# Decoder trunk kernel: dilated heads scored in pairs with weight parts dealt anew, forget gates loaded with the value columns, expert sums and closing norm by tile, three output transfers

## The reference

```python
def hybrid_mixer(x, ...):                       # head groups: 4 MLA, 6 FoX, 6 dilated
    h = x @ w_in
    c_q, c_kv, k_rope, fox_qkv, fox_f, dil_qkv = jnp.split(h, cuts, axis=-1)
    ...
    log_f = jax.nn.log_sigmoid(fox_f.astype(jnp.float32) + b_forget.astype(jnp.float32))
    cum_log_f = jnp.cumsum(log_f, axis=1).transpose(0, 2, 1)
    o_b = causal_block_attention(q_b, k_b, v_b, cum_log_f)
    ...
    o_c = dilated_mixture_attention(rope(q_c, positions), rope(k_c, positions), v_c)
    return mixed @ w_out

def reference(...):
    for l in range(DEPTH):
        x = layer_norm(DEEPNORM_ALPHA * x + mix, ln_mix_g[l], ln_mix_b[l])
        xa = memory_cross_attention(x, mem, xattn_w_q[l], xattn_w_kv[l], xattn_w_o[l])
        x = layer_norm(DEEPNORM_ALPHA * x + xa, ln_mem_g[l], ln_mem_b[l])
        gates = shared_group_router(x, router_w, router_bias)
        ff = moe_ffn(x, gates, expert_w_gate[l], expert_w_up[l], expert_w_down[l])
        x = layer_norm(DEEPNORM_ALPHA * x + ff, ln_ffn_g[l], ln_ffn_b[l])
    return x
```

## Time and profile before

| | us |
|---|---|
| three timed runs: median (lowest to highest) | 868.74 (868.0 to 871.59) |
| the profiled execution's own time | 867.3 |
| its span in the trace | 865.7 |
| TensorE busy | 816.2 (94%) |
| VectorE busy | 628.9 (73%) |
| ScalarE busy | 503.0 (58%) |
| GpSimd busy | 89.9 (10%) |

### The profile page before, as it was taken

The page is one execution under the profiler, slowest core; times in us unless marked ns, Lnnn a source line. Parts: engine busy times, 40 slices in busy tenths (PEclk is TensorE's granted clock), DMA queues, the critical chain, the costliest instruction groups (busy, mean ns, idle before and its releaser), DMA issues.

```text
span 865.7 us, 12257 instructions
## 1 busy us (share of the span) xinstructions
PE 816.2 (94%) x4411; PEld 695.0 (80%) x4411; DVE 628.9 (73%) x1094; ACT 503.0 (58%) x794; POOL 89.9 (10%) x165
## 2 busy tenths in 40 slices
PE   6998899899998999999999989999999989999993
PEld 6997798679876888888889978867898768888882
DVE  4656766775657899999565577666856589999984
ACT  3655554454435788888355646544443467888871
POOL 3156200030000000000020530000200100000001
PEclk9999999999999999999999999999999999999997
DMA  9953353455333699999465524425533439999941
GB/s 275 337 178 111 128 163 106 139 160 190 94 121 121 218 366 370 364 369 372 159 181 166 180 98 146 148 97 195 196 120 100 128 118 306 366 367 366 367 147 49
DMA packets 124110, 177.06 MB, mean 205 GB/s; under 512 B 12320, under 2 KB 92720, under 8 KB 124048
## 3 DMA queue, kind: packets, MB, share of 16 engines
q1 hardware_dynamic: 122064, 169.56, 58.8%
q0 software_dynamic: 1984, 6.70, 2.6%
...
## 4 chain that ended last, share of the span: by engine, by line
PE 81%; DVE 10%; ACT 3%; issue 3%; DMA 1%; POOL 1%; SPq 0%; DVEq 0%; ACTq 0%; POOLq 0%
PE bank L1489 21%; PE bank L1491 21%; PE bank L1490 21%; DVE w_split L490 2%; PE bank L1766 2%; PE bank L1618 2%; PE bank L1659 2%; PE bank L1607 2%; PE bank L1629 1%; PE bank L1596 1%; PE bank L1650 1%; DVE xT_lo L997 1%; DVE p_sb L1046 1%; PE bank L1606 1%; DMA xs<-in_x_dram 1%
## 5 line engine op out<-in xcount | busy, mean ns | idle before, releaser
L490 DVE TENSOR_TENSOR w_split<-raw,w_split 128x1024 fp32r<-128x1024 f32 (+2 forms) x336 | 386.9, 1174 | 74.5 <-ACT w_split L485 69.9
L485 ACT ACTIVATE w_split<-raw 128x1024 fp32r<-128x1024 f32 (+2 forms) x336 | 335.5, 1010 | 111.7 <-PE bank L1491 97.5
L1489 PE MATMUL bank<-w_split,xg_hi 128*128 128x512 f32 x256 | 103.5, 404 | 0.0
L1491 PE MATMUL bank<-w_split,xg_lo 128*128 128x512 f32 x256 | 100.2, 392 | 0.0
L1490 PE MATMUL bank<-w_split,xg_hi 128*128 128x512 f32 x256 | 100.2, 391 | 0.0
L1489 PE MATMUL bank<-w_split,xT_hi 128*128 128x384 f32 (+1 forms) x224 | 77.8, 347 | 2.0 <-DVE w_split L490 1.6
L1491 PE MATMUL bank<-w_split,xT_lo 128*128 128x384 f32 (+1 forms) x224 | 75.7, 338 | 0.0
L1490 PE MATMUL bank<-w_split,xT_hi 128*128 128x384 f32 (+1 forms) x224 | 75.6, 338 | 0.0
L602 POOL TENSOR_SCALAR st<-st 128x1 f32<-128x1 f32 x12 | 5.7, 473 | 653.4 <-ACT junk L748 653.0
L707 ACT ACTIVATE qkT<-bank 66x512 f32<-66x512 f32 (+2 forms) x32 | 19.0, 593 | 80.0 <-PE bank L1596 80.0
L1491 PEld LDWEIGHTS bank<-w_split,xg_lo 128*128 128x128 f32 x256 | 48.1, 188 | 11.0
...
## 6 DMA issues: line engine op xcount, KB each, us to landing
raw<-in_expert_w_gate_dram SPq DMA_DIRECT2D x128, 256.0 KB, 5.0
raw<-in_expert_w_up_dram SPq DMA_DIRECT2D x128, 256.0 KB, 6.7
...
```

The costliest lines, as they stand in the source:

```text
L485: nc.scalar.activation(w_hi[:, i % SPL, 0:w], raw[:, i % RAW, 0:w], ACT.Copy).then_inc(hi_ready, 1)
L490: nc.vector.tensor_tensor(w_lo[:, i % SPL, 0:w], raw[:, i % RAW, 0:w], w_hi[:, i % SPL, 0:w].bitcast(F32), ALU.subtract).then_inc(lo_ready, 1)
L1489: nc.tensor.matmul(o, lhs[0], rhs[0], start=first, stop=False, skip_group_check=shared)
L1491: return nc.tensor.matmul(o, lhs[1], rhs[0], start=False, stop=last, skip_group_check=shared)
```

## The change

It has four parts. (1) The forget-gate columns, which lie behind FV's, are loaded with FV, not with A; FV comes before FK and FQ; `fz` is made from FV's banks and waited for only in the LT job. (2) The dilated heads 10 to 15 are taken in pairs: one set of transposes turns query and key of both heads (128 columns), one `head_scores` makes both heads' scores, from partitions 0 to 63 and 64 to 127, in banks `B_S` and `B_QK`; `slots` and the stream are dealt anew; VectorE divides before `evac_o`. (3) At a layer's end tile 0's sums are finished and signalled ahead of those of groups 2 and 3 of tile 1, the choice for overfull groups (`overflow`) stands ahead of the last groups, and the two tiles are added and normalized one by one, the last in halves. Parts A0 and A1 of the next layer are split before the last expert outputs are evacuated. (4) The result leaves in three transfers.

Cut to its core:

```diff
     for l in range(n_layers):
-for name, js in (("A", range(4)), ("FQ", range(4)), ("FK", range(4)), ("FV", range(2)), ("UQ", range(1)),
-                 ("UKV", range(1)), ("FV", range(2, 4)), ("DQ", range(4)), ("DK", range(4)), ("DV", range(4)),
-                 ("MK0", range(4)), ("MK1", range(4)), ("MV0", range(4)), ("WO0", range(4)), ("WO1", range(4)),
+for name, js in (("A", range(4)), ("FV", range(4)), ("FK", range(4)), ("FQ", range(2)), ("UQ", range(1)),
+                 ("UKV", range(1)), ("FQ", range(2, 4)), ("DQ", range(4)), ("DK", range(4)), ("DV", range(4)),
+                 ("MK0", range(4)), ("MK1", range(4)), ("MV0", range(4)), ("WO0", range(3)), ("WO1", range(1)), ("WO0", range(3, 4)), ("WO1", range(1, 4)),
                  ("MV1", range(4)), ("XQ0", range(4)), ("XQ1", range(4)), ("XO0", range(4)), ("XO1", range(4)),
...
-slots = [3] + [2] * 2 + [1] * 7 + [2] * 6 + [1] * 3
+slots = [3, 2, 2] + [2, 1] * 4 + [1, 2] * 2 + [1] * 4
 turns, ahead_of = [], []
...
     assert len(turns[l]) == HEADS + 3
-    ahead_of.append(turns[l][1:] + [[index[l, "WO0", 3], index[l, "WO1", 0]]])
+    ahead_of.append(turns[l][1:] + [[index[l, "WO1", 0], index[l, "WO0", 3]]])
+
+def in_pair(h):
+
+    return MLA_H + FOX_H <= h < HEADS
+
+def qk_slot(h):
+
+    return (h // 2 + 1) % 2 if in_pair(h) else h % 2
...
-    return B_QK if h >= HEADS and (h - HEADS) % 2 else B_S
+    return B_QK if (in_pair(h) or h >= HEADS) and (h - HEADS) % 2 else B_S
+
+def scored(s):
+
+    if in_pair(s - 1):
+        return (s - 1, s) if s % 2 else ()
+    return (s - 1,) if 1 <= s <= HEADS else ()
...
+    sp.wait_ge(x_ready.sem, x_ready.at(L - 1, 5))
+    sp.dma_start(out[0][0:P, :], xs[:, 0, :]).then_inc(out_sent, 16)
+    sp.wait_ge(end_half.sem, end_half.at(L - 1, 1))
+    sp.dma_start(out[0][P:2 * P, 0:DM // 2], xs[:, 1, 0:DM // 2]).then_inc(out_sent, 16)
     sp.wait_ge(x_ready.sem, x_ready.at(L - 1, 6))
-    sp.dma_start(out[0].rearrange("(t p) d -> p t d", p=P), xs[:, :, :]).then_inc(out_sent, 16)
-    sp.wait_ge(out_sent, 16)
+    sp.dma_start(out[0][P:2 * P, DM // 2:DM], xs[:, 1, DM // 2:DM]).then_inc(out_sent, 16)
+    sp.wait_ge(out_sent, 48)
...
-            nc.scalar.activation(kf[:, t, :], b[:, QR + KVR:A_ALL], ACT.Copy).then_inc(job_a.sem, 1)
-        for i in range(first + 8, first + 10):
+            nc.scalar.activation(kf[:, t, :], b[:, QR + KVR:A_W], ACT.Copy).then_inc(job_a.sem, 1)
+        for i in range(first + 8, first + 12):
             split_hi(act, i)
-
-        act.wait_ge(fz_v.sem, fz_v.at(l, 2))
+        copy_job(l, "FV", lambda t: fv[:, t, :, 0:HD], lambda b: heads_of(b, FOX_H, HD))
+
+        act.wait_ge(fz_v.sem, fz_v.at(l, 1))
         nc.scalar.activation(fz[:, 2, :], fz[:, 1, :], ACT.Exp, scale=-1.0).then_inc(fz_a.sem, 1)
...
         nc.scalar.activation(fz[:, 3, :], fz[:, 2, :], ACT.Ln, bias=1.0).then_inc(fz_a.sem, 1)
-        for i in range(first + 10, first + 12):
-            split_hi(act, i)
-        copy_job(l, "FQ", lambda t: fq[:, t, :, 0:HD], lambda b: heads_of(b, FOX_H, HD))
         for i in range(first + 12, first + 14):
...
         aT_of(l, NE - 1, 1)
+        if l + 1 < L:
+            for j in range(2):
+                split_hi(act, index[l + 1, "A", j])
...
                                                gains[:, c0:c0 + w], ALU.mult, ALU.mult).then_inc(job_v.sem, 1)
-        z3 = lambda i: fz[:, i, :].rearrange("p (t f) -> p t f", t=TT)
-        nc.vector.tensor_tensor(z3(0), kf[:, :, ROPE:], bforget[:, :].unsqueeze(1).to_broadcast([P, TT, FOX_H]),
-                                ALU.add).then_inc(fz_v.sem, 1)
-        dve.wait_ge(fz_v.sem, fz_v.at(l, 1))
+        for i in range(first + 8, first + 12):
+            split_lo(dve, i)
+        for t, b in enumerate(banks("FV")):
+            dve.wait_ge(job_a.sem, job_a.at(l, evac_a[job["FV"]] - 1 + t))
+            nc.vector.tensor_tensor(fz[:, 0, t * FOX_H:(t + 1) * FOX_H], b[:, FOX_H * HD:FOX_H * HD + FOX_H],
+                                    bforget[:, :], ALU.add).then_inc(job_v.sem, 1)
+        dve.wait_ge(job_v.sem, job_v.at(l, evac_v[job["FV"]]))
         nc.vector.scalar_tensor_tensor(fz[:, 1, :], fz[:, 0, :], -1.0, fz[:, 0, :], ALU.mult, ALU.max).then_inc(fz_v.sem, 1)
-        for i in range(first + 8, first + 10):
-            split_lo(dve, i)
+        split_lo(dve, first + 12)
         dve.wait_ge(fz_a.sem, fz_a.at(l, 2))
...
             .then_inc(fz_v.sem, 1)
-        for i in range(first + 10, first + 14):
-            split_lo(dve, i)
+        split_lo(dve, first + 13)
...
-                softmax_max(l, s - 1)
+            for h in scored(s):
+                softmax_max(l, h)
+            if in_pair(s - 1) and s % 2 == 0:
+                softmax_norm(l, s - 1)
             if 2 <= s <= HEADS + 1:
                 evac_pT(l, s - 2)
+            if 1 <= s <= HEADS and not (in_pair(s - 1) and s % 2 == 0):
+                softmax_norm(l, s - 1)
             if s >= 3 and (s - 3) % 2 == 1:
...
                 evac_o(l, s - 3)
-            if 1 <= s <= HEADS:
-                softmax_norm(l, s - 1)
...
                 dve.nop().then_inc(s_.sem, s_.per)
-        add_experts(l)
+        add_experts(l, 0)
         scale(l, 2, 0)
-        rest_of_norm(l, 2)
+        add_experts(l, 1)
+        norm_x(l, 2, 0)
+        scale(l, 2, 1)
+        norm_halves(l, 2, 1, end_half)
...
         d = MLA_D if h < MLA_H else FOX_D if h < MLA_H + FOX_H else DIL_D
-        if h >= MLA_H + FOX_H:
+        if in_pair(h):
+            pe.wait_ge(s_masked.sem, s_masked.at(l, 2 * h))
             pe.nop().then_inc(paused_t, 1)
...
                 c0 = (2 * n + t) * P
-                ins = nc.tensor.transpose(B_QK[0:d, c0:c0 + P], v[:, t, g, :], ident[:, :])
-        ins.then_inc(qk_done.sem, 1)
+                if in_pair(h):
+                    ins = nc.tensor.transpose(B_QK[:, c0:c0 + P], v[:, t, g:g + 2, :].rearrange("p h d -> p (h d)"),
+                                              ident[:, :])
+                else:
+                    ins = nc.tensor.transpose(B_QK[0:d, c0:c0 + P], v[:, t, g, :], ident[:, :])
+        ins.then_inc(qk_done.sem, 2 if in_pair(h) else 1)
...
     def head_scores(l, h):
-        if h < HEADS:
+        if in_pair(h):
+            pe.wait_ge(qkT_ready.sem, qkT_ready.at(l, h + 2))
+            pe.wait_ge(s_masked.sem, s_masked.at(l, 2 * h))
+            for q, k in ((slice(0, P), slice(0, P)), (slice(P, T), slice(P, 3 * P))):
+                for i in range(2):
+                    v = qkT[i * DIL_D:(i + 1) * DIL_D, qk_slot(h), :]
+                    ins = nc.tensor.matmul(score_bank(h + i)[:, k], v[:, q], v[:, T:T + k.stop - k.start],
+                                           start=True, stop=True)
+            ins.then_inc(s_done.sem, 2)
+        elif h < HEADS:
...
                                            stop=g == NG - 1 and v is y_lo, skip_group_check=True)
-        if t == TT - 1 and g == NG - 1:
+        if g == NG - 1:
             ins.then_inc(summed.sem, 1)
...
         if l:
-            keep_busy(27)
+            keep_busy(20)
         if l == 0:
...
         if l:
-            keep_busy(3)
+            keep_busy(5)
+            pe.wait_ge(end_half.sem, end_half.at(l - 1, 1))
+            for f in range(KC):
+                if f == KC // 2:
+                    pe.wait_ge(x_ready.sem, x_ready.at(l, 0))
+                ins = nc.tensor.transpose(banks("XT1")[f // 4][:, (f % 4) * P:(f % 4 + 1) * P],
+                                          xs[:, 1, f * P:(f + 1) * P], ident[:, :])
+                if f == KC // 2 - 1:
+                    ins.then_inc(begin_turned, 1)
+            ins.then_inc(turned.sem, 1)
+            keep_busy(11)
         else:
             pe.wait_ge(x_in[1], 16)
-        turn_x(l, "XT1", 1, 0)
-        if l:
-            keep_busy(11)
-        else:
...
-        pe.wait_ge(job_v.sem, job_v.at(l, evac_v[job["A"]]))
-        pe.wait_ge(fz_v.sem, fz_v.at(l, 3))
         open_job(l, "FK")
...
                 nc.tensor.transpose(b[:, k * P:(k + 1) * P], lat[:, t, k * P:(k + 1) * P], ident[:, :])
+            if t == 0:
+                pe.wait_ge(fz_v.sem, fz_v.at(l, 2))
...
         experts_down(l, NE - 1)
-        scatter(l, 1, range(NG - 1))
-        scatter(l, 0, [NG - 1])
-        scatter(l, 1, [NG - 1])
+        scatter(l, 1, range(2))
         over = overflow(pe, l, paused_t)
...
         with pe.If(over < 1):
-            for s_, n in ((ov_gathered, 1), (ov_upped, EPG), (ov_turned, EPG), (ov_used, EPG), (summed, 1)):
+            for s_, n in ((ov_gathered, 1), (ov_upped, EPG), (ov_turned, EPG), (ov_used, EPG)):
                 pe.nop().then_inc(s_.sem, n)
+        scatter(l, 0, [NG - 1])
+        scatter(l, 1, range(2, NG))
```

128 lines of the change are left out of this document (69 added, 59 removed), and 2 rows, old and new, of the table jobs.

## The result

The changed kernel took 839.9 us (median of four runs, 836.44 to 842.83) beside 869.18 for the kernel before on the same chip: a ratio of 0.966, 95% interval 0.961 to 0.970. The forecast was 845.5 us. The profiled execution of it took 841.01 us with a span of 839.4, 26.3 us less than the 865.7 of before, where the working had 22.9.

What follows compares the result with a forecast made beforehand. TensorE, 94% busy, was taken to bound the kernel. Gains of 14.9 (heads), 1.5, 0.5, 2.4 and 3.6 sum to 22.9 us, taking the profiled 867.3 to 844.4; with 1.4 us for the median, 845.5 us was predicted, range 839 to 853.

Steps and rivals of the forecast that it cites:

- more comes back than I count: Rival: double scores and start better than taken, end of the heads' loop clean, 840 us; chance 0.07.
- the sum for the heads: Attention heads of both layers: gains less losses give 7.45 us in a layer, 14.9 us in all.
- Turns dealt anew: Head turns 3 to 9: second parts in odd turns remove TensorE's waits for the division; 4.5 us a layer (2.5 to 5.0).
- Scores in pairs: Six dilated heads: three shared transposes and double scores of 1.0 us each save 3.2 us a layer (1.1 to 4.2).
- A new wait: Transposes of heads 10 and 11: TensorE waits for the masks behind head 9's scores, 1.15 us lost a layer.
- End of the loop: Last head turns: 1.6 us idle for 2.86, gain 1.2 us (0 to 2.9), less 0.3 for VectorE's addition.
- Forget gates and start: Earlier FK without the `fz_v` wait, 1.5 us (0.5 to 1.9); small gate transfers gone at the start, 0.5 us.
- gain 0.5 us: Kernel start: the small transfer ahead of token tile 1 on SyncE goes, 0.46 us; nothing at least, 1.5 us at most.
- The chain through ScalarE: Forget gates: exponential and logarithm end 7.0 us after FV, hidden behind FK's 8.3 us, with 1.3 us to spare.
- End of a layer: First layer's end: earlier sums, norm by tile and early splits start the next layer sooner; 2.4 us (1.5 to 2.9).
- result 3.6 us: Last layer's end: normalization 1.7 us earlier and a shorter last transfer, 1.9 us; 3.6 us (2.5 to 4.2).
- The clock: Rival: TensorE's clock falls in the dilated turns and stays down, slower than before, above 873 us; chance 0.02.

Runs made afterwards that it cites:

- the deal alone: Kernel before with only the parts dealt anew and WO1_0 ahead of WO0_3, heads scored one by one: 862.37 us beside 867.68.
- part 1 alone: Kernel before with only the forget-gate columns moved to FV, FV ahead of FK and FQ, no small pieces at the start: 868.98 us beside 867.68.
- parts 3 and 4 alone: Kernel before with only sums and closing norm by tile, A0 and A1 split early, three output transfers: 863.06 us beside 867.68.

## Why the prediction was right, and where it was not

The measured 839.9 us is not at the forecast but at the rival "more comes back than I count", 840 us, to which I gave 0.07. Of its three reasons one held in full (the double scores), one in part (the end of the loop, 0.97 us idle where "clean" would be none), and one not (the start brought no time). The largest single share, 1.9 us in both layers for stops that are gone, stood in none of them. The step that was mis-sized is the sum for the heads: 14.9 us, and the traces show 20.2.

- **Turns dealt anew, 4.5 us in a layer.** Right: 4.64 and 4.96 us of the 4.96 went. But the deal alone is worth 3.4 us in the heads, and 5.0 on top of the pairs.
- **Scores in pairs, 3.2 us.** The mechanism was right, the size low. By the starts in the trace the dilated heads' scores and their transposes of query and key took 7.35 us in a layer and now take 3.74: 3.6 us. The term of 1.0 us for a double score was mis-sized: 0.88 us on average over the three, practically one head's 0.85. The rule of the Trainium skill that was weighed against it (TensorEngine Tiling, Theoretical Speedup), up to twice the speed, would as an estimate have given 3.7.
- **A new wait, 1.15 us.** 1.48 and 1.12 us, at the place that was named; and needless.
- **End of the loop, 1.6 us idle.** 0.97 us, so 1.9 us were gained, not 1.2; the 0.3 us that I had set against it, for VectorE's addition behind WO0_3, do not show.
- **What the sum left out**: each stop of TensorE costs some 0.17 us beyond what stands in brackets, since in a row of products each starts some 0.17 us before the shown end of the one ahead (384 columns: shown as 0.33 us, starts 0.17 us apart), and after a stop it cannot. Five or six stops fewer are 0.9 to 1.0 us in a layer. Together: heads 9.7 and 10.5 us where the sum had 7.45, 5.3 us too little. The 1.17 us behind the first layer's heads are luck, the slow instruction of the execution before.
- **Forget gates and start, 1.5 + 0.5 us.** The step "gain 0.5 us", that only the one small piece ahead of tile 1 counts, failed in its form: the first product came 4.9 us sooner (2.6 between the means), and of the 4.9 4.1 were lost again, since ScalarE takes FV3's split only at 23.59, waiting for its data, and the memory's copy, the sine's table and A's squares are queued behind:

```profile
23.59 0.86 ACT L501 ACTIVATE w_split<-raw 128x780 fp32r<-128x780 f32 x1 [1.45 <-DMA raw<-in_w_in_dram]
```

  The earlier first product of FK, 1.2 us (34.6 for 35.92 is 1.3), came as 1.57 from `lat` on, but not in form: I expected no pause ahead of FK, and one of 2.12 us is there, because FV's products end sooner too. Start and gates together were worth 1.7 us at FK by my terms, 2.3 in this pair of executions and 1.6 between the means; what failed is that FK then runs at full clock, and 1.5 us went there in five of six executions. The chain through ScalarE stayed hidden, as I had said: VectorE's last step on `fz` ends at 39.99 us, and LT's products, from 43.50 on, wait for nothing. As time, the whole part is worth nothing measurable.
- **End of a layer 2.4, result 3.6 us.** 2.4 and 3.7, and 1.97 for the three transfers alone. The mechanism is as worked out: the first addition starts 2.3 us behind `y_lo` and not 4.0, and TensorE goes from its useless products into the next layer's first product without a wait.
- **The clock.** The rival was placed in the dilated turns. One profiled execution with those heads did fall there, right behind the 1.48 us at head 10 (117.0 to 120.4 us, with one transfer of the result), and the first layer's heads took 1.4 us more; it did not stay down. With the old heads it fell more often, at the end of the loop: in three of the six layers of the kernel before and of the kernels with part 1 alone and with parts 3 and 4 alone. What I had not seen is that the number of falls differs in each execution. They took 4 us more from the profiled one than from that of before. So the 26.3 us for my 22.9 hold 5.3 us more from the heads, 1.2 by the slow instruction of before, 4 less through the clock, and 0.9 of small differences.
